# A gated recurrence over two blocks of tokens: the second block receives the first through its state instead of through an eighth level of products

## The reference

```python
def step(S, inp):                       # per chunk of the prompt; S is the state, 64 x 64 per head
    qi, bi, ki, vi = inp                # bi: cumulated log of the forget gate
    diff = bi[:, :, :, None, :] - bi[:, :, None, :, :]
    decay = jnp.exp(jnp.where(causal[:, :, None], diff, NEG_BIG))
    att = jnp.einsum('bhtc,bhsc,bhtsc->bhts', qi, ki, decay)
    o = jnp.einsum('bhts,bhsv->bhtv', att, vi) + jnp.einsum('bhtc,bhcv->bhtv', qi * jnp.exp(bi), S)
    bl = bi[:, :, -1:, :]
    S = jnp.exp(bl)[:, :, 0, :, None] * S + jnp.einsum('bhsc,bhsv->bhcv', ki * jnp.exp(bl - bi), vi)
    return S, o
```

## Time and profile before

| | |
|---|---|
| median of 3 runs | 806.99 us (806.79 to 807.72) |
| the profiled execution | 807.15 us |
| its span, first to last instruction | 805.3 us |
| granted TensorE clock, mean | 0.997 of full speed (2.4 GHz) |
| busy: TensorE, VectorE, ScalarE, GpSimd | 796.5, 565.8, 437.3, 274.0 us |
| DMA | 199.75 MB, mean 248 GB/s |

### The profile page before, as it was taken

How to read it: one execution, slowest core, us unless ns; L and a number is a source line. 1 busy time by engine, 2 the same in 40 slices (tenths; PEclk the granted TensorE clock), 3 DMA queues, 4 the chain that set the end, 5 groups by cost and what they waited for, 6 DMA issues and landing times.

```text
span 805.3 us, 17669 instructions
## 1 busy us (share of the span) xinstructions
PE 796.5 (99%) x6780; PEld 783.9 (97%) x6780; DVE 565.8 (70%) x774; ACT 437.3 (54%) x629; POOL 274.0 (34%) x246
## 2 busy tenths in 40 slices
PE   8999999999999999999999999999999999999996
PEld 8999999999999999999999999999999999999996
DVE  6978798577877665554587788966797676645552
ACT  6665567554666665444354646665455666634442
POOL 3599393056700000122149817702663000001220
PEclk9999999999999999999999999999999999999998
DMA  8797879968567588767558968997766767787751
GB/s 323 215 341 282 309 234 314 254 228 297 183 210 260 189 292 284 252 238 251 191 174 219 372 260 279 267 260 254 265 228 209 226 227 251 241 281 249 248 208 54
DMA packets 126036, 199.75 MB, mean 248 GB/s; under 512 B 19643, under 2 KB 115691, under 8 KB 118507
## 3 DMA queue, kind: packets, MB, share of 16 engines
q1 hardware_dynamic: 124682, 196.48, 73.8%
q10 hardware_dynamic: 1296, 2.48, 0.8%
HBM read 191.03 MB, written 51.90 MB: 302 GB/s over the span
## 4 chain that ended last, share of the span: by engine, by line
PE 98%; DVE 1%; DMA 1%; ACT 0%; DVEq 0%; ACTq 0%; issue 0%
PE main L693 29%; PE main L694 28%; PE main L695 28%; PE small L695 1%; PE small L694 1%; PE small L693 1%; PE small L738 1%; PE small L709 1%; DMA raw<-in_w_in 1%; PE main L678 1%; PE main L679 0%; PE main L682 0%; PE main L669 0%; PE small L933 0%; PE small L725 0%; PE main L665 0%
## 5 line engine op out<-in xcount | busy, mean ns | idle before, releaser
L1048 ACT ACTIVATE w_hi<-raw 128x1024 fp32r<-128x1024 f32 (+1 forms) x256 | 266.3, 1042 | 230.7 <-PE main L695 132.7
L1304 DVE TENSOR_TENSOR w_lo<-raw,w_hi 128x1024 fp32r<-128x1024 f32 (+1 forms) x256 | 337.6, 1320 | 64.8 <-ACT w_hi L1048 63.1
L693 PE MATMUL main<-h_hi,w_hi 128*128 128x264 f32 x1248 | 357.3, 286 | 0.0
L694 PE MATMUL main<-h_lo,w_hi 128*128 128x264 f32 x1248 | 353.7, 283 | 0.0
L695 PE MATMUL main<-h_hi,w_lo 128*128 128x264 f32 x1248 | 353.4, 283 | 0.0
L693 PEld LDWEIGHTS main<-h_hi,w_hi 128*128 128x128 f32 x1248 | 235.0, 188 | 3.1 <-issue 2.1
L694 PEld LDWEIGHTS main<-h_lo,w_hi 128*128 128x128 f32 x1248 | 235.2, 188 | 0.1
L695 PEld LDWEIGHTS main<-h_hi,w_lo 128*128 128x128 f32 x1248 | 234.0, 188 | 0.0
L693 PE MATMUL main<-a_hi,w_hi 128*128 128x264 f32 x512 | 145.3, 284 | 0.0
L694 PE MATMUL main<-a_lo,w_hi 128*128 128x264 f32 x512 | 145.0, 283 | 0.0
L695 PE MATMUL main<-a_hi,w_lo 128*128 128x264 f32 x512 | 145.0, 283 | 0.0
(11 more groups left out here) (253 smaller groups left out, 1029.9 us busy)
## 6 DMA issues: line engine op xcount, KB each, us to landing
raw<-in_w_in SPq DMA_DIRECT2D x48, 1024.0 KB, 5.7
raw<-in_w_up SPq DMA_DIRECT2D x32, 1024.0 KB, 5.3
raw<-in_w_down SPq DMA_DIRECT2D x32, 1024.0 KB, 5.3
out_kvs<-in_cache SPq DMA_DIRECT2D x48, 512.0 KB
out_kvs<-in_cache SPq DMA_DIRECT2D x32, 496.0 KB
raw<-in_w_o SPq DMA_DIRECT2D x8, 1024.0 KB, 5.8
raw<-in_w_br SPq DMA_DIRECT2D x8, 768.0 KB, 6.1
gates<-q_scratch SPq DMA_DIRECT2D x4, 768.0 KB, 7.6
```

The costliest lines, as they stand in the source:

```text
L693: pe.matmul(out[:, 0:TOK], wh, rh, start=start and k == 0, stop=False)
L694: pe.matmul(out[:, 0:TOK], wh, rl, start=False, stop=False)
L1048: act.activation(w_hi[:, slot(l, u), 0:k, :], raw_of(u, k), ACT.Copy).then_inc(w_hi_ready, 1)
L1304: dve.tensor_tensor(w_lo[:, slot(l, u), 0:k, :], raw_of(u, k), w_hi[:, slot(l, u), 0:k, :].bitcast(F32), ALU.subtract).then_inc(w_lo_ready, 1)
```

## The change

The eighth level is no longer multiplied. In its place the keys of the first block are weighed to the end of their own block instead of to the end of the prompt (GpSimd leaves out the last doubling of `suf_f` and the keys of level 8). TensorE multiplies each block's keys and values to a state of its own (`block states`), ScalarE copies the first block's state to `first_state`, and in the recurrence the second block multiplies its queries, weighed from the start of the block (still the queries of level 8), by this state. The last state becomes the first one times the decay of the second block plus the second one, on VectorE.

The places: the transposes of the decayed keys go from the stop after unit 19 to the stop after 17, and their copy on ScalarE from turn 20 to 18; the block states stand after 19, before the scores; the recurrence moves from the stop after 19 to the stop after 21, before the second half of the scores, and its copy from turn 20 to 22; the copy of the state in turn 24 goes. `TURNS` has two names fewer and another order, and `probs` and `probs_t` change places in memory.

```diff
-LEVELS_AT = ((10, (2, 3)), (12, (4, 5)), (14, (6,)), (17, (7, 8)))
+LEVELS_AT = ((10, (2, 3)), (12, (4, 5)), (14, (6,)), (17, (7,)))
 TURNS = (
-    + ["values T"] + [f"level {i} {h}" for i in range(7, 9) for h in range(2)]
-    + ["decayed keys T", "sample rows T", "recurrence", "scores 0 0", "scores 1 0"]
-    + ["scores 0 1", "scores 1 1", "sample states"]
-    + ["state", "sample recurrence", "attention values T 0", "attention values T 1"]
+    + ["values T"] + [f"level 7 {h}" for h in range(2)] + ["decayed keys T"]
+    + ["sample rows T", "block states", "scores 0 0", "scores 1 0"]
+    + ["recurrence", "scores 0 1", "scores 1 1", "sample states"]
+    + ["sample recurrence", "attention values T 0", "attention values T 1"]
...
 # TensorE, between
-                if u == 19:
+                if u == 17:
                     pe.wait_ge(final_keys, l + 1)
                     transposes(l, "decayed keys T", ...)
+                if u == 19:
+                    pe.wait_ge(roped, l + 1)
                     pe.wait_ge(s_cols_ready, l * 3 + 3)
                     transposes(l, "sample rows T", ...)
+                    pe.wait_ge(v_tm_ready, l + 1)
+                    pe.wait_ge(k_tm_ready, l + 1)
+                    bank = use_bank(pe, l, "block states")
+                    for tb in range(2):
+                        for hp in range(2):
+                            for h in range(2):
+                                rows = slice(h * HD, (h + 1) * HD)
+                                c = (tb * 2 + hp) * HD
+                                mm = pe.matmul(bank[rows, c:c + HD], k_tm[:, tb, hp, rows], v_tm[:, tb, hp, rows],
+                                               start=True, stop=True)
+                    done(mm, "block states")
+                    pe.wait_ge(q_classes_ready, l + 1)
+                    scores(l, 0)
+                if u == 21:
                     pe.wait_ge(masked, l * 20 + 20)
-                    pe.wait_ge(far_ready, 2 * l + 2)
-                    pe.wait_ge(v_tm_ready, l + 1)
+                    pe.wait_ge(level_ready, l * 8 + 8)
+                    pe.wait_ge(first_state_ready, l + 1)
                     bank = use_bank(pe, l, "recurrence")
...
-                            pe.matmul(bank[rows, c + P:c + 2 * P], v_tm[:, 0, hp, rows], att_far[:, h, hp, :],
-                                      start=True, stop=False)
+                            pe.matmul(bank[rows, c + P:c + 2 * P], first_state[rows, hp, :],
+                                      queries_of(8)[rows, hp, P:2 * P], start=True, stop=False)
...
-                    pe.wait_ge(q_classes_ready, l + 1)
-                    scores(l, 0)
-                if u == 21:
                     scores(l, 1)
                     sample_states(l)
                 if u == 23:
-                    pe.wait_ge(k_tm_ready, l + 1)
-                    bank = use_bank(pe, l, "state")
...
 # ScalarE, between
                 if u == 18:
-                    for h in range(2):
-                        copy_bank(l, f"level 8 {h}", att_far[:, h, :, :]..., far_ready)
+                    copy_bank(l, "decayed keys T", k_tm[...]..., k_tm_ready)
...
                     copy_bank(l, "sample rows T", ...)
-                    copy_bank(l, "decayed keys T", k_tm[...]..., k_tm_ready)
+                    copy_bank(l, "block states", first_state[...]..., lambda b: b[:, 0:2 * HD], first_state_ready)
+                if u == 22:
                     act.wait_ge(silu_ready, l + 1)
                     copy_bank(l, "recurrence", o_c[:, :, 0:PROMPT], ...)
-                if u == 24:
-                    act.wait_ge(states_stored, l * STATE_STORES * 16 + 16)
-                    copy_bank(l, "state", state_p[...]..., state_p_ready)
...
 # VectorE, turn 20, behind mask_scores(0)
+                    if u == 20:
+                        dve.wait_ge(states_stored, l * STATE_STORES * 16 + 16)
+                        dve.wait_ge(first_state_ready, l + 1)
+                        bank = take(dve, l, "block states")
+                        for hp in range(2):
+                            ins = dve.scalar_tensor_tensor(state_p[:, hp, :], first_state[:, hp, :],
+                                                           cum_f[:, hp, PROMPT - 1:PROMPT],
+                                                           bank[:, (2 + hp) * HD:(3 + hp) * HD], ALU.mult, ALU.add)
+                        ins.then_inc(state_p_ready, 1)
...
 # GpSimd, the loop over levels
-                        for tb in range(2 if i < 8 else 1):
+                        for tb in range(2 if i < 8 else 0):
...
                     pool.sem_inc(level_ready, 1)
+                    if i == 8:
+                        continue
```

More of the change, by code:

```diff
@@ L293, in trunk @@
         masked = sem("masked")
-        far_ready = sem("far_ready")
+        first_state_ready = sem("first_state_ready")
         outer_ready = sem("outer_ready")
@@ L871, in between @@
                 if u == 23:
-                    pe.wait_ge(k_tm_ready, l + 1)
-                    bank = use_bank(pe, l, "state")
-                    for hp in range(2):
-                        for h in range(2):
[L876 to L880, removed]
                     sample_rows(l)
@@ L1128, in between @@
                 if u == 18:
[L1129 to L1132, removed]
+                    copy_bank(l, "decayed keys T", k_tm[:, :, :, :].rearrange("p t h c -> p (t h c)"),
+                              lambda b: b[:, :], k_tm_ready)
+                    freed("decayed keys T", k_tm_ready, l + 1)
                 if u == 19:
@@ L1141, in between @@
                     freed("sample rows T", s_rows_copied, l + 1)
-                    copy_bank(l, "decayed keys T", k_tm[:, :, :, :].rearrange("p t h c -> p (t h c)"),
-                              lambda b: b[:, :], k_tm_ready)
-                    freed("decayed keys T", k_tm_ready, l + 1)
+                    copy_bank(l, "block states", first_state[:, :, :].rearrange("p h c -> p (h c)"),
+                              lambda b: b[:, 0:2 * HD], first_state_ready)
+                if u == 22:
                     act.wait_ge(silu_ready, l + 1)
@@ L1148, in between @@
                     freed("recurrence", o_prompt_ready, l + 1)
-                if u == 24:
-                    act.wait_ge(states_stored, l * STATE_STORES * 16 + 16)
-                    copy_bank(l, "state", state_p[:, :, :].rearrange("p h c -> p (h c)"),
-                              lambda b: b[:, 0:2 * HD], state_p_ready)
-                    freed("state", state_p_ready, l + 1)
                 if u == 26:
@@ L1542, in _ @@
                         mask_scores(0)
+                    if u == 20:
[7 more added lines that the diff above has]
+                        ins.then_inc(state_p_ready, 1)
+                        dve.wait_ge(state_p_ready, l + 1)
+                        dve.sem_inc(bank_taken[TURN["block states"] % 4], 1)
                     if u == 22:
@@ L1777, in _ @@
                                             cum[:, :, 1, half - 1:half].to_broadcast([P, n, half]), ALU.mult))
-                    if i < 8:
-                        step(pool.tensor_tensor(cum[:, :, 1, :], cum[:, :, 1, :],
-                                                cum[:, :, 0, half - 1:half].to_broadcast([P, n, half]), ALU.mult))
+                    step(pool.tensor_tensor(cum[:, :, 1, :], cum[:, :, 1, :],
+                                            cum[:, :, 0, half - 1:half].to_broadcast([P, n, half]), ALU.mult))
                 take(pool, l, "level 5 1")
```

17 lines of the change are left out of this document (8 added, 9 removed).

## The result

The changed kernel takes 810.65 us in the median of 6 runs (810.06 to 811.00), beside 807.08 us for the kernel before in the same series (806.79 to 807.74). The ratio is 1.0042, with a 95% interval of 1.0031 to 1.0053: **3.6 us slower**. The forecast was 811.0, its range 808.7 to 812.8. The profiled execution of the changed kernel took 810.06 us, with a span of 808.3 us (before: 807.15 and 805.3) at a granted TensorE clock of 0.998 (before: 0.997), so the clock explains nothing here.

The account below looks back on a forecast made before the run. TensorE, busy 99% of the span, was taken as the bound. Stops of 3.3 - 0.05 - 1.46 - 0.49 = +1.3 us per layer, +2.6 for two, plus a 1.4 us wait gave 811.0 us, range 808.7 to 812.8.

Parts of the forecast that it names:

- The price of a change of depth: TensorE, inside an accumulation: each change costs about 0.09 us over the pitch of 0.11, either way.
- the nine groups: Recurrence, stop after 21: eight changes of depth between groups, 0.36 us a group, the last 0.38; 3.3 us in all.
- Rival 2: Recurrence, stop after 21: state product shares the array without emptying it, pitch kept; 806.5 us, 807.9 with layer 0's wait; chance 0.07.
- B: The recurrence's product with the state, 64 deep and 64 wide, two passes per head half, between products 128 deep.
- The stops after 17 and 23: TensorE: level 8 out and transposes in, -0.05 us; state product out, next product's weights +0.03, sum -0.49 us.
- After 19: TensorE stop: transposes leave -0.44, recurrence leaves -1.75, block states with change to the scores +0.73; sum -1.46 us.
- The wait in layer 0: TensorE's block states wait for VectorE's masks, held up by GpSimd's earlier samples' state product: about 1.4 us, between 0 and 1.9.
- The relief: VectorE, layer 0: one rope product, held by 0.33 us by a GpSimd operation that goes, is freed.
- "nothing": Layer 1: GpSimd runs 5 us earlier against TensorE, masks end well ahead in either order, so no wait.
- What was costed at nothing: VectorE's two last-state products (0 to 1.25 us), GpSimd's keys (ready 65.8, wanted 67.9), ScalarE's first-state copy: no TensorE wait.
- rival 1: GpSimd's samples' state product falls after the last split before the masks, no layer 0 wait; 809.6 us (808.7 to 810.9); chance 0.28.
- The 0.9 us of wait: Layer 0 wait used in the forecast's own lower bound: 1.7 + 0.9, giving 809.6 us.

Follow-up runs that it names:

- four_joints: Changed kernel with the recurrence grouped by pair of heads (first-block, state, then second-block products of both heads), four changes of depth instead of eight; 808.01 us.
- deep: Changed kernel with the first state laid out 128 rows deep, zeros in the other head's rows, same order of products; 808.66 us.
- s_late: Changed kernel with GpSimd's product on the samples' states waiting in addition for VectorE's masks of level 7; 809.34 us.
- regroup: Changed kernel with the recurrence reordered: four state products first, then the eight value products, heads alternating; 807.18 us.
- state_last: Changed kernel with s_late's edit, value products first and the recurrence's state products behind the second scores; 805.74 us.

## Why the prediction was right

**The bound and the method held.** Between its start and its end TensorE shows one wait, the one in layer 0. The changes at the four stops and the one wait add up to 3.3 us, and the span grew by 3.0.

**The price of a change of depth held, and it decided the sign.** Forecast 0.36 for a group, the new rows show 0.36 to 0.37; forecast 3.3 for the nine groups, measured 3.27. It was read from other changes, one of depth at 2 columns and one of columns alone, and it carried over. The Trainium skill, TensorE: Matmul & The Clock Gate, Step-by-step, gives the drain some 128 cycles; by the estimate that the forecast made from it the sum would have been 16 x 0.04 = 0.64 us smaller (the forecast rounded this to 0.7). The trace decides for the rows: three changes more cost 0.45 us in four_joints, 0.15 each, of which 0.09 are the change. Rival 2 (B shares the array and keeps the pitch) fell on the trace of the changed kernel, and deep shows what it would have been worth: 1.54 us in each layer.

**The stops after 17 and 23 held** to 0.02 us (-0.05 and -0.51). **After 19 one term was mis-sized**: the block states were put at +0.73 with the change to the scores and measured 0.62 (470.07 to 470.69). The forecast added 0.52 us, read up to the start of the next group, and the whole 0.22 from a last pass to the next shape on top. But the 0.52 already holds the pitch of the last pass, 0.06, and behind these short passes the next shape comes 0.15 after the last one, not 0.22 (470.54 to 470.69, from the pass starts of the trace). So only 0.62 - 0.52 = 0.10 should have been added. That is most of the 1.3 against 1.12 per layer.

**The wait in layer 0 held in place, cause and layer; its size was off, and two of its steps came out otherwise.** The forecast was 1.4, the measured wait 1.04. Its steps, one by one. The product of GpSimd was to start at about 71 and started at 70.24. It was to hold the rope sum or the split by up to 1.8: it held the split by 2.96 - 1.21 = 1.75. The relief was put at 0.33, from the first rope product, and this is the first step that failed: that gain was eaten on the way, since the split at 67.42, now beside the silu gate, took 2.22 us where it had taken 1.64, and VectorE came to the rope sum at 69.91 as before (69.88). The relief came from the rope sum itself, which before had been held to 2.58 us (beside the gate), took 1.81 now, and gave 0.77. What the gate would hold once it moved was not in the forecast. So the masks moved by 0.03 - 0.77 + 1.75 = 1.01 us (73.52 to 74.53), not by 1.5. The second step that failed: TensorE needed the bank of the first mask alone and went on at 75.16, 0.13 before the second mask ended, where the forecast let it wait for both. On the other side it came to the block states at 73.93 + 0.20 = 74.13 instead of 74.5, mostly because this execution was ahead. So the release, forecast at 75.8, came at 75.16, 0.64 sooner, and the need 0.37 sooner: 0.27 less than the 75.8 - 74.5 = 1.3 that the forecast had rounded up to 1.4.

s_late shows the cause, not only the place: with the GpSimd product alone moved, split, masks and block states are all back in time. For layer 1 the forecast said that GpSimd is 5 us earlier against TensorE; at this product it is 8.6 (0.38 us ahead of the last pass of unit 19 in layer 0, 73.83 against 74.21; 8.94 in layer 1, 459.05 against 467.99), which makes its "nothing" only safer. The Trainium skill, SBUF — State Buffer, "SBUF: two separate sides", says that VectorE and GpSimd share a pair of ports as an exclusive lock, held for the whole instruction by whichever starts first, when VectorE's operation has two inputs in SBUF and GpSimd's reads SBUF. The rows agree: first the GpSimd product stretches beside the rope sum (3.29 us instead of 1.94), then the split beside the product (2.96 instead of 1.21).

**What was costed at nothing was nothing.** The two products for the last state took 0.46 us together (the bound was 0 to 1.25), ahead of a long recurrence; no wait at the second scores. The keys ended at 61.92 + 3.80 = 65.7 (forecast 65.8), 1.9 us ahead of their transposes. No wait of TensorE for ScalarE's copy of the first state. The other runs show how far this cover reaches: in regroup, with a recurrence of 1.61 us, the two products end at 84.01 + 0.46 = 84.47, 0.17 ahead of the second scores, and there is still no wait; in deep, with 1.15 us of products and a recurrence of 1.7 us, it failed by 0.46.

**The range.** 810.65 lies in it, 0.35 below the forecast, and rival 1, the next in chance, has its upper bound at 810.9: the time alone would not have parted the two. The wait in layer 0 does. The counted sums were too high at both terms (0.18 per layer and 0.36 for the wait, together 0.7); the medians differ by 0.3 more than the traces' account, which hides part of it. That the forecast lies so near is in this part luck. The 0.9 us of wait in the forecast's own lower bound has no working beside it.

## What to carry to other kernels

Count the changes of shape on TensorE (rows and columns of the array that the weights take), not only its passes: the same 24 passes took 3.27 us interleaved, 2.06 in pairs and 1.61 with one change, and a product put where its shape already stands pays no joint at all. A product made deeper with zeros can be cheaper than a small one between large ones. And work taken from an engine off the critical path moves everything behind it on that engine forward: ask beside which operation of the other engine it then falls, since one line that puts it back (s_late) was worth 1.3 us.

## What the hardware showed that was not expected

- A group of four 64-column passes on the two column halves of the array costs as much up to the next shape as a group of two on one half (0.36 to 0.37 us in four_joints, 0.36 in the changed kernel). Between changes of shape, the second head rides along for nothing.
- Passes 64 x 64 of another product, with other operands and another bank, join without a gap: in state_last, scores and state together take 83.69 to 84.73 = 1.04 us, where the 16 scores alone took 0.60 with the change behind them in regroup. The eight state passes cost 0.44 us, 0.055 each.
- VectorE and GpSimd held each other in turn in one stretch: 1.35 us lost by GpSimd's product, and then 1.75 us lost by VectorE's split behind it.
